# Two modulations computed from half rows beside the first experts, and bias and minimum of the hybrid attention in one pass

## What is computed

```python
c_lat = jax.nn.silu(c)[:, None, :]
c_con = jax.nn.silu(c_ctx)[None, None, :]
for i in range(DEPTH):                                             # DEPTH = 2
    mod_l = jnp.split(c_lat @ ada_w[i] + ada_b[i], N_MOD, axis=-1)  # six vectors of 1024
    mod_c = jnp.split(c_con @ ada_w[i] + ada_b[i], N_MOD, axis=-1)
    h_lat = modulate(rmsnorm(x, norm_mix_g[i]), mod_l[0], mod_l[1])
    ...
    x = x + mod_l[2] * o_lat                                       # the mixer's output
    h_lat = modulate(rmsnorm(x, norm_ffn_g[i]), mod_l[3], mod_l[4])
    x = x + mod_l[5] * expert_choice_ffn(h_lat, moe_router[i], ...)
...
# differential attention of the second block, q and k normalised per head and half
s = jnp.einsum('bqhmd,bkhmd->bhmqk', qb, kb).astype(jnp.float32) * scale
s = s + jnp.transpose(bias, (2, 0, 1))[None, :, None]
s = jnp.where(dist[None, None, None] >= 0, s, -1e30)
p = jax.nn.softmax(s, axis=-1)
w = p[:, :, 0] - lam * p[:, :, 1]
```

## Time and profile before

| | |
|---|---|
| device time, median of 3 runs | 2554.59 us (2550.34 to 2562.33) |
| the profiled execution: time, span | 2560.84 us, 2559.1 us |
| TensorE busy, mean granted clock | 2428.8 us (95%), 0.983 |
| VectorE, ScalarE, GpSimd busy | 1201.3, 423.6, 304.5 us |
| moved by DMA | 597.11 MB, mean 233 GB/s |

### The profile page before, as it was taken

The page is one execution under the profiler, slowest core; times in us unless marked ns, Lnnn a source line. Parts: engine busy times, 40 slices in busy tenths (PEclk is TensorE's granted clock), DMA queues, the critical chain, the costliest instruction groups (busy, mean ns, idle before and its releaser), DMA issues. The chain is left out here.

```text
span 2559.1 us, 53520 instructions
## 1 busy us (share of the span) xinstructions
PE 2428.8 (95%) x23863; PEld 1767.1 (69%) x23863; DVE 1201.3 (47%) x2185; ACT 423.6 (17%) x963; POOL 304.5 (12%) x262
## 2 busy tenths in 40 slices
PE   7999999899999998999999999888899989999999
PEld 4587665677777664588887654444467758888888
DVE  5785655511111115777686333323265566445632
ACT  2132541300000001200243000000011342210000
POOL 0010001022222220000001000000040302340000
PEclk9999999899999999999999999999999979999999
DMA  8472325799999996454307999999942210222220
GB/s 322 151 246 89 128 83 197 304 369 405 407 407 407 406 408 263 169 188 118 114 18 293 388 422 421 422 423 421 421 166 93 85 55 28 83 89 93 107 91 33
DMA packets 79889, 597.11 MB, mean 233 GB/s; under 512 B 10564, under 2 KB 17668, under 8 KB 34556
## 3 DMA queue, kind: packets, MB, share of 16 engines
q1 hardware_dynamic: 62540, 552.00, 54.0%
q0 software_dynamic: 14384, 31.20, 4.5%
q10 hardware_dynamic: 2736, 10.49, 1.0%
HBM read 576.50 MB, written 17.41 MB: 232 GB/s over the span
## 5 line engine op out<-in xcount | busy, mean ns | idle before, releaser
L1787 PE MATMUL moe_ps<-room,moe_xs 128*32 128x256 f32 x9568 | 537.0, 383 | 46.2 <-DMA room<-in_experts 42.6
L1787 PEld LDWEIGHTS moe_ps<-room,moe_xs 128*32 128x32 f32 x9568 | 355.6, 111 | 226.9 <-issue 40.4
L1787 PE MATMUL moe_ps<-room,moe_hid_t 128*32 128x256 f32 x4432 | 248.5, 382 | 5.6 <-DMA room<-in_experts 5.3
L1787 PEld LDWEIGHTS moe_ps<-room,moe_hid_t 128*32 128x32 f32 x4432 | 160.5, 111 | 95.1 <-issue 15.0
L2061 DVE SCALAR_TENSOR_TENSOR x_feat<-moe_ps,mod,x_feat 128x512 f32<-128x512 f32 (+1 forms) x144 | 95.9, 730 | 135.3 <-PE moe_ps L1861 124.9
L777 PE MATMUL hout_ps<-h_feat,room 128*128 128x256 f32 x696 | 159.1, 380 | 0.0
L2128 DVE TENSOR_TENSOR moe_hid<-moe_hid,moe_ps 128x512 f32<-128x512 f32 x32 | 22.0, 688 | 279.0 <-PE moe_ps L1787 279.0
L777 PEld LDWEIGHTS hout_ps<-h_feat,room 128*128 128x128 f32 x696 | 132.3, 190 | 18.5 <-issue 0.5
L2148 DVE TENSOR_SCALAR moe_y<-moe_ps,moe_gates 128x256 f32<-128x256 f32 x42 | 17.7, 478 | 265.4 <-PE moe_ps L1787 265.4
L2004 ACT ACTIVATE moe_hid<-moe_ps 128x512 f32<-128x512 f32 x32 | 19.1, 597 | 741.6 <-PE moe_ps L1787 706.9
L1833 POOL DMA_INDIRECT acc<-moe_y,moe_sum_ids x42 | 69.6, 1657 | 292.6 <-DVE moe_y L2148 284.0
(11 more groups left out here) (695 smaller groups left out, 3777.5 us busy)
## 6 DMA issues: line engine op xcount, KB each, us to landing
room<-in_experts SPq DMA_DIRECT2D x140, 2048.0 KB, 30.5
room<-in_experts SPq DMA_DIRECT2D x67, 1024.0 KB, 22.5
moe_slot<-in_experts SPq DMA_DIRECT2D x30, 1024.0 KB, 41.3
room<-in_ffn_gate SPq DMA_DIRECT2D x9, 1024.0 KB, 4.8
room<-in_ffn_down SPq DMA_DIRECT2D x6, 1408.0 KB, 7.0
room<-in_ada_first SPq DMA_DIRECT2D x8, 1024.0 KB, 13.1
qk_ada_w<-in_ada_w SPq DMA_DIRECT2D x8, 1024.0 KB, 5.0
room<-in_ada_t POOLq DMA_DIRECT2D x16, 512.0 KB, 8.9
```

Of the source, the lines that this page charges most:

```text
L1787: mm = pe.matmul(group_ps(part, g)[32 * q:32 * q + 32], turned[:, k * GROUP:(k + 1) * GROUP], weights[:, m, q], start=(k == 0 and g != 1), ...
```

## The change

It has two parts that don't touch each other.

The first: modulations (0, 3) and (0, 5) are no longer made by TensorE's side work in the q and k projection and in the output projection. (0, 3) takes the place of (1, 0) among the early row modulations. (0, 5) and (1, 0) are made in the first expert stage by a new class, `HalfRows`: rows cut into halves of 512 columns, 32 tiles of 256 KB in 16 pairs, which ScalarE's queue loads, one pair behind each Silu; VectorE multiplies and sums each for both conditions, one pair behind each expert's transpose. The first half of the columns gives a partial sum, the second starts from it. Each half of the two condition rows is loaded as a broadcast and put through a Silu. The first product of a pass goes to the last PSUM bank, which the end of the stage needs, so TensorE waits for all tiles there.

The second: in the hybrid attention the root mean square of q is spread and multiplied into q as that of k is, with the negative scale, so that the scores come out negated. The bias is negated too. A single instruction adds the bias and keeps the minimum over the row, and ScalarE's exponential takes the negative of its input. The reduction over both halves, the transposes of `root` and `rq` go.

```diff
-ROW_PARTS = [(1, n) for n in range(N_MOD)]
-ROWS_EARLY = 2
+SIDE_PARTS = [(0, 2), (0, 4)]
+ROW_PARTS = [(0, 3), (1, 1), (1, 2), (1, 3), (1, 4), (1, 5), (0, 5), (1, 0)]
+ROWS_EARLY, ROWS_KEYS = 2, 6
...
+class HalfRows:
+    HALF = D // 2
+    def __init__(self, nc, ctx, K, dram, parts, product):
...
+        self.tiles = [(half, layer, part, n) for half in range(2) for layer, part in parts for n in range(KT)]
...
+    def load_pair(self, act, pair):
+        sig = self.sig
+        m = 2 * pair
+        if m >= len(self.tiles):
+            return
+        if m:
+            act.wait_ge(sig["used"], m)
+        half = self.tiles[m][0]
+        columns = slice(half * self.HALF, (half + 1) * self.HALF)
+        begins = m % self.each == 0
+        if begins:
+            for r in range(2):
+                act.dma_start(self.cond[:, r], bass.AP(self.dram["cond_rows"].tensor, r * D + half * self.HALF,
+                                                       [[0, P], [1, self.HALF]])).then_inc(sig["cond"], 16)
+        for room in range(2):
+            _, layer, part, n = self.tiles[m + room]
+            act.dma_start(self.rooms[:, room], self.dram["ada_t"][ROW_PARTS.index((layer, part)) * KT + n][:, columns]
+                          ).then_inc(sig[f"landed_{room}"], 16)
+        if begins:
+            act.wait_ge(sig["cond"], 32 * (half + 1))
+            act.activation(self.cond[:], self.cond[:], ACT.Silu).then_inc(sig["silu"], 1)
+
+    def work_pair(self, dve, pair):
+        K, sig = self.K, self.sig
+        for room in range(2):
+            m = 2 * pair + room
...
+            dve.wait_ge(sig["silu"], half + 1)
+            dve.wait_ge(sig[f"landed_{room}"], 16 * (pair + 1))
...
+            for r, product in enumerate((self.product, tile)):
+                so_far = self.sums[:, r, i:i + 1]
+                begin, to = (so_far, K.mod[:, layer, r, KT * part + n, :]) if half else (
+                    K.col("ada_b", 48 * layer + KT * part + n), so_far)
+                dve.tensor_tensor_reduce(product, tile, self.cond[:, r], 1.0, begin, ALU.mult, ALU.add, to
+                                         ).then_inc(sig["used" if r else "products"], 1)
...
@@ experts_stage, TensorE, behind the last up product
                         pe.wait_ge(sig["silu"], EXPERTS)
+                        pe.wait_ge(mods.sig["used"], len(mods.tiles))
                         spread(LATE, batches[0], True, False)
@@ experts_stage, ScalarE
+                    if mods:
+                        mods.load_pair(act, 0)
                     gate(0)
+                    if mods:
+                        mods.load_pair(act, 1)
                     for e in range(LAST):
...
                         gate(e + 1)
+                        if mods:
+                            mods.load_pair(act, e + 2)
@@ experts_stage, VectorE
+                        if mods and e == 0:
+                            mods.work_pair(dve, 0)
                         dve.wait_ge(sig["w_used"], used_up(e, UP))
...
                         dve.transpose(hid_t[:].rearrange("p g c -> p (g c)"),
                                       hid[:].rearrange("p g c -> p (g c)")).then_inc(sig["hid_t"], 1)
 
+                        if mods and e < LAST:
+                            mods.work_pair(dve, e + 1)
@@ mlstm_attention
-                     add_gated(K, 0, 0), make="begun", mods=[(0, 5)], pieces_at=(9, 13, 17, 21), turned_at=3, ps=ps,
+                     add_gated(K, 0, 0), make="begun", ps=ps,
@@ mlstm_projections
-            seven(nc, K, dram, "qk", feed, K.h, halves, evacuate, mods=[(0, 2), (0, 3)], after=convolve_now,
+            seven(nc, K, dram, "qk", feed, K.h, halves, evacuate, mods=[(0, 2)], after=convolve_now,
@@ hybrid_mixers, TensorE
+                def spread_q(h):
+                    if h >= 2:
+                        pe.wait_ge(sig["q_scaled"], h - 1)
+                    else:
+                        pe.wait_ge(sig["z_abs"], 1)
+                    pe.matmul(ps[:, 6 + h % 2], T["back"][group(h), 3], root[group(h)], start=True,
+                              stop=True).then_inc(sig["q_spread"], 1)
...
-                for i in range(LT):
-                    mm = pe.transpose(ps[:, 6, i * P:(i + 1) * P], root[:, i * P:(i + 1) * P], K.ident[:])
-                mm.then_inc(sig["q_turned"], 1)
                 spread_k(0)
+                spread_q(0)
                 spread_k(1)
+                spread_q(1)
                 values(3)
-                spread_k(2)
-                spread_k(3)
-
-                pe.wait_ge(sig["k_scaled"], 1)
+                for h in range(2, H):
+                    spread_k(h)
+                    spread_q(h)
+
+                pe.wait_ge(sig["q_scaled"], 1)
                 scores(0)
-                pe.wait_ge(sig["k_scaled"], H)
+                pe.wait_ge(sig["q_scaled"], H)
@@ hybrid_mixers, ScalarE
-                    act.wait_ge(sig["top"], u + 1)
                     for m in range(2):
                         sv = s[:, u % 3, m, 0:(i + 1) * P]
-                        act.activation(sv, sv, ACT.Exp, bias=top[:, u % 2, m:m + 1],
+                        act.wait_ge(sig["biased"], 2 * u + m + 1)
+                        act.activation(sv, sv, ACT.Exp, bias=low_most[:, u % 2, m:m + 1], scale=-1.0,
                                        accum_out=total[:, u % 2, m:m + 1]).then_inc(sig["exp"], 1)
@@ hybrid_mixers, VectorE
                     dve.scalar_tensor_tensor(f[:, H + h], f[:, H + h], gain[:], ps[:, 4 + h % 2], ALU.mult,
                                              ALU.mult).then_inc(sig["k_scaled"], 1)
+                    dve.wait_ge(sig["q_spread"], h + 1)
+                    dve.scalar_tensor_tensor(f[:, h], f[:, h], -DA_QK ** -0.5, ps[:, 6 + h % 2], ALU.mult,
+                                             ALU.mult).then_inc(sig["q_scaled"], 1)
...
                         dve.wait_ge(sig["scores"], 2 * u + m + 1)
-                        dve.scalar_tensor_tensor(s[:, u % 3, m, 0:n], ps[:, 2 + 2 * (u % 2) + m, 0:n], rq[:, i * H + h, m:m + 1],
-                                                 bias[:, h, n0:n0 + n], ALU.mult, ALU.add).then_inc(sig["biased"], 1)
+                        dve.tensor_tensor_reduce(s[:, u % 3, m, 0:n], ps[:, 2 + 2 * (u % 2) + m, 0:n], bias[:, h, n0:n0 + n], 1.0,
+                                                 3.0e38, ALU.add, ALU.min, low_most[:, u % 2, m:m + 1]).then_inc(sig["biased"], 1)
                     if u >= 1:
                         weights(u - 1)
-                    dve.wait_ge(sig["biased"], 2 * u + 2)
-                    dve.tensor_reduce(top[:, u % 2], s[:, u % 3, :, 0:n], AX_X, ALU.max, negate=True).then_inc(sig["top"], 1)
```

More of the change, by code:

```diff
@@ L383, in work @@
                                              1.0, K.vec[:, g:g + KT, 0], ALU.add, ALU.mult)
+class HalfRows:
+    HALF = D // 2
+    def __init__(self, nc, ctx, K, dram, parts, product):
+        self.K, self.dram, self.product = K, dram, product
+        sb = lambda n, s: ctx.enter_context(nc.sbuf_tensor(f"half_rows_{n}", s, F32))
+        self.cond, self.rooms = sb("cond", [P, 2, self.HALF]), sb("tiles", [P, 2, self.HALF])
+        self.each = KT * len(parts)
+        self.sums = sb("sums", [P, 2, self.each])
+        self.tiles = [(half, layer, part, n) for half in range(2) for layer, part in parts for n in range(KT)]
+        self.sig = Signals(nc, "half_rows")
+    def load_pair(self, act, pair):
[23 more added lines that the diff above has]
+            m = 2 * pair + room
+            half, layer, part, n = self.tiles[m]
+            i, tile = m % self.each, self.rooms[:, room]
+            dve.wait_ge(sig["silu"], half + 1)
+            dve.wait_ge(sig[f"landed_{room}"], 16 * (pair + 1))
+            if half:
+                dve.wait_ge(sig["used"], m - self.each + 1)
+            if m >= 1:
+                dve.wait_ge(sig["products"], m)
+            for r, product in enumerate((self.product, tile)):
[4 more added lines that the diff above has]
+                                         ).then_inc(sig["used" if r else "products"], 1)
@@ L2561, in mlstm_attention @@
         mout = Seven(nc, ctx, K, dram, "mout", feed, o, four_sums((K.h[:].rearrange("p k t -> p (k t)"), 4, TOK // 2)),
-                     add_gated(K, 0, 0), make="begun", mods=[(0, 5)], pieces_at=(9, 13, 17, 21), turned_at=3, ps=ps,
+                     add_gated(K, 0, 0), make="begun", ps=ps,
                      rooms=(work[:, 0:4 * TOK], work[:, 4 * TOK:6 * TOK]), lead=((0, 1), (0, 5), (1, 1)), ready=ready,
-                     side={"room": work[:, 8 * TOK:8 * TOK + 2 * D].rearrange("p (q n) -> p q n", q=2),
-                           "row": work[:, 8 * TOK + 2 * D:8 * TOK + 2 * D + D // 4], "bank": ps[:, 7]},
                      beside={"scalar": squares, "gpsimd": add_squares, "sync_with": load_beside,
@@ L3101, in retention_layer @@
                 plan += [(("rv", c, "u"), 1), (("rv", c, "c11"), 1)]
```

(8 more changed lines are left out.)

24 lines of the change are left out of this document (11 added, 13 removed).

## The result

The changed kernel takes 2567.76 us (median of 11 runs, 2564.59 to 2572.78) against 2558.34 for the kernel before on the same chip (11 runs, 2550.34 to 2562.79): a ratio of 1.0039, 95% interval 1.003 to 1.0048, so +7.7 to +12.3 us, where the forecast's sum was +8. The profiled execution of the changed kernel has a span of 2563.9 us and 2565.74 in all. That the sum comes out doesn't show that its terms do.

TensorE's timeline in the q and k projection, against the earlier trace rows.

The account below looks back on a forecast made before the run. The prediction took TensorE to bound most of the kernel and the DMA engines to set the first expert stage's end. Terms -9 + 20 - 3 = +8 gave 2562.6 on the median 2554.59, stated as 2563, range 2550 to 2578.

Parts of the forecast that it names:

- The bound: First expert stage: the DMA engines, not TensorE, set its end, so added transfers lengthen it.
- Landing times: Sign in the first expert stage: the weights' time to landing should reach 35 us well before 860.
- Part 1: Q and k and output projections: 8 pieces of side work leave TensorE, -9 us, bounds 5 to 10 saved.
- the lower bound: Projections: only 5 us saved if VectorE holds the second half of the first projection.
- Part 2: First expert stage: half-row transfers lengthen it by 20 us, bounds 16 to 31; VectorE's passes are hidden.
- both terms, 25 and 5: First expert stage: 36 transfers cost 25 us of full DMA engines, of which idle engines absorb some 5.
- the rule of 512 B: Half-tile transfers: 2 KB rows would cost what the weights cost, term 17.5; the prediction held the rows against it.
- Rival (b): Expert stage: each half tile costs the full 0.85 us, none absorbed; +18.6 in all, 2573 us; chance 0.20.
- rival (a): Expert stage: the half rows are hidden, costing 0 to 6; -6 to -12 in all, 2545 us; chance 0.12.
- Part 3: Hybrid attention: spreads cost 1.7 us, VectorE saves 9.0 but only partly counts; -3 us, bounds +2 to -7.
- 4.5 (3.5 and 1 of clock): Hybrid attention from 2042 to 2062: VectorE's shorter units save 3.5 us, and 1 us of lost clock is given back.
- rival (c): Projections gain only 2 or the hybrid loses its 2: +13 to +15 in all, 2569 us; chance 0.08.

Follow-up runs that it names:

- e5: Changed kernel loading only the first pair of half tiles, all 64 passes run on it: 2549.18 us, ratio 0.9964 to the kernel before.
- e2: Changed kernel with the hybrid attention of before, so only the modulation edits: 2566.54 us, ratio 1.003 to the kernel before.
- e4: Changed kernel with one product of the values moved to where TensorE waits for VectorE's scaling: 2561.47 us, ratio 1.0013 to the kernel before.
- e6: Changed kernel with all tiles loaded but each VectorE pass cut to two columns: 2567.49 us, ratio 1.0048 to the kernel before.
- e11: Changed kernel with each of the 32 half tiles loaded twice: 2590.71 us, ratio 1.0122 to the kernel before.
- e7: Changed kernel with each pair of half tiles loaded as one 512 KB tile in rows of 4 KB: 2564.9 us, ratio 1.0029 to the kernel before.
- e1: Kernel before plus only the hybrid attention's edits: 2560.96 us, ratio 1.0008 to the kernel before.
- e3: Kernel before plus the hybrid attention's edits, one product of the values moved into TensorE's wait: 2555.54 us, ratio 0.9988 to the kernel before.
- e8: Changed kernel, product of the values moved, all 32 half tiles and their passes beside the first attention: 2581.01 us, ratio 1.009 to the kernel before.
- e10: Changed kernel, values moved, only (1, 0) by half rows, beside the attention; (0, 5) stays on TensorE: 2547.81 us, ratio 0.9962 to the kernel before.
- e12: Changed kernel, values moved, 16 half tiles beside the attention and 16 beside the output projection: 2554.1 us, ratio 0.9979 to the kernel before.

## Why the prediction was right

The forecast of +8 us was right, by terms whose errors cancel, and that they cancel is luck. In absolute time it gave 2563 against 2567.76; 3.75 us of this are the kernel before, whose median over 11 runs lies that much above the three runs that the forecast started from.

**The bound.** That the DMA engines set the end of the expert stage was the step on which the sign hung, and e5 shows it. Landing times reached 37.5 us by 860, as the prediction asked, and no long wait of VectorE for a tile came.

**Part 1, -9.** Measured -10: 5.0 in the q and k projection, 5.0 in the output projection (stretch B). VectorE held neither projection back, as the lower bound had feared for the first. A piece with its share of the turns and copies gave 1.25 us (10 / 8), where 1.10 were read between two products.

**Part 2, +20.** Measured +17.0 (567.3, the mean of e2, e4 and e6, against 550.3, the mean of four kernels without tiles), and +19.0 in the changed kernel's profiled execution, with the low clock at the stage's start. The price of a tile, taken as 25 / 36 = 0.69, is 0.64 by bytes and 0.67 by e11. By these 36 transfers cost 23 to 24, and 6 to 7 of them were absorbed: both terms, 25 and 5, made the sum 1 to 2 us too high. The prediction said that the rows of this case speak against the rule of 512 B for line rate (the Trainium skill, page "DMA: Bandwidth & Descriptors", section "Specifications"). For this stage they didn't: both rows came from other stretches, without the experts' weights beside them, and in the stage e7 finds rows of 4 KB at most 0.9 us cheaper over 32 tiles. By the rule the term was 17.5, and 17.0 is measured. Rival (b) took the lone tile's 0.85 and falls with e11; rival (a), with e5.

**Part 3, -3.** Measured about 0 (stretch E) and +2 (-0.8 to +4.6) by e1. The spreads cost 1.2, not 1.7: from start to start the four of q take 1.73 (the two groups of spreads 1.92 and 1.93, 1.06 each before), and the transposes' 0.53 went. VectorE saved 12.2, not 9.0, in part since the new pass is shorter than the old one (485 ns against 544). The second half gave back 4.0 where the forecast had 4.5 (3.5 and 1 of clock): TensorE was 3.2 us late against before, counted from the mixers' start, at the product at 2051.7, and 0.8 early at their end. The step that failed is "VectorE scales q in four passes of 0.745, 3.0 us; they hide in the 3.1 us that it waits for the bias transfer". They hide for VectorE. TensorE waits for them too, 1.60 us where it waited 1.07 before, and the clock falls behind it. The 0.5 us and the 1.7 to 2.5 of lost clock are most of the missing 3 us. With a product moved into the wait (e3, e4) the mixers take 123.1 against 126.1 for the old ones, the mean of two: the forecast's -3, though e8, with the same attention, needs 124.7. Of rival (c) the half that concerned the hybrid is what happened, but not its +13, since Parts 1 and 2 came out lower.

**The sum.** -10 + 17.0 + 0 to 2 = +7 to +9, up to 1.7 more where the clock is low at the stage's start, and perhaps 1.7 less by stretch D. Measured is +9.4 (7.7 to 12.3). The terms are known to some 2 us, no closer.

## What to carry to other kernels

On full DMA engines price a new transfer by its bytes at the core's whole rate, not by how long it takes when alone, and look for its place where the share is low. An engine's idle share isn't enough to hide work on it: ask at each place who waits behind it. Here 27 us of passes cost 0.5 us in front of a wait of their engine, and 54 us at three places of each head cost 33, with tiles that came late and loads of ScalarE's function table among it. Side work needs its inputs early, too: with the same two places for tiles no pass waited in e10, and some did in e8 and e12. Where an edit lengthens a chain that one engine hands to another, count the waits at both ends, and what a wait does to TensorE's clock, which can cost as much as the wait itself.

## What the runs showed of the hardware

- A wait of 1.60 us, with TensorE busy 2.40 of 4.00 us around it, was followed by a granted clock of 0.58 for 4 us; in e1, 0.50 to 0.53 for 6. In the kernel before, a wait of 1.07 us at the same place (1.93 of 3.00 busy) was not. Eight matmuls to no use in the wait kept it at 1.00. The length of a wait alone doesn't tell: at the start of the experts a wait of 2.17 us was followed by 0.66 for 5 us (the changed kernel, e11), one of 2.32 us (e1) by 1.00.
- In the expert stage the rate of the full DMA engines, 407 GB/s, did not depend on the mix of packets: 7553, 8731 or 9530 packets in 160 us moved the same 65.15 to 65.17 MB. That isn't a rate for rows of 2 KB alone: such rows by themselves took 96.2% of the engines for 0.65 MB in 2 us.
- The pass that adds and keeps the minimum over 512 columns, one operand from TensorE's banks, takes 0.68 us with 0.08 for its read; 0.29 over 128 columns.
- A load of ScalarE's function table took 1.28 us, and one stood before and one behind the Silu of the conditions in e8 (337.38 and 339.74).
